# Three feed-forward stages run their first gate block on x before the norm's factor, and GpSimd forms low parts of weights

## The reference

```python
mod = c_act @ mod_w[i] + mod_b[i]                 # nine rows of 1024: shift, scale, gain, three times
h = modulate(rmsnorm_2(x, norm_g[i, 0]), sh1, sc1)   # h * (1 + scale) + shift
x = x + FFN_RES * g1[:, None, :] * swiglu_2(h, ffn_w13[i, 0], ffn_w2[i, 0])

def swiglu_2(h, w13, w2):
    a, b = jnp.split(h @ w13, 2, axis=-1)
    return (jax.nn.silu(a) * b) @ w2
```

## Time and profile before

| | us |
|---|---|
| device time, median of 3 runs | 1616.53 (1615.57 to 1620.67) |
| profiled execution, span | 1619.2 |
| PE busy | 1605.0 (99%) |
| DVE busy | 1221.3 (75%) |
| ACT busy | 807.2 (50%) |
| POOL busy | 48.4 (3%) |

### The profile page before, as it was taken

One profiled execution on the slowest core, in us unless ns is written; L12 is line 12 of the kernel. 1 busy time (PEld: TensorE's weight loads), 2 busy tenths in 40 slices (PEclk: granted clock), 3 DMA queues, 4 the chain that ended last, 5 costly groups with the idle time before them and its releaser, 6 DMA issues.

```text
span 1619.2 us, 33790 instructions
## 1 busy us (share of the span) xinstructions
PE 1605.0 (99%) x14157; PEld 1583.5 (98%) x14157; DVE 1221.3 (75%) x1382; ACT 807.2 (50%) x892; POOL 48.4 (3%) x81
## 2 busy tenths in 40 slices
PE   9999999999999999999999999999999999999998
PEld 9999999999999999999998999999999998899998
DVE  6888786676778878887777888877889578774544
ACT  5434567654644354443567654445444466654343
POOL 0000000000000000000000000000000010000000
PEclk9999999999999999999999999999999999999999
DMA  8788544444568865888453368874798535345551
GB/s 327 289 305 306 219 175 171 150 156 160 184 255 294 311 224 209 316 326 295 153 183 130 131 246 327 304 292 160 288 342 316 195 139 197 135 157 206 183 197 63
DMA packets 51066, 365.04 MB, mean 225 GB/s; under 512 B 5792, under 2 KB 5920, under 8 KB 7072
## 3 DMA queue, kind: packets, MB, share of 16 engines
q1 hardware_dynamic: 40176, 287.03, 48.5%
q0 software_dynamic: 10368, 75.50, 12.8%
q10 hardware_dynamic: 432, 1.20, 0.2%
HBM read 362.65 MB, written 1.05 MB: 225 GB/s over the span
## 4 chain that ended last, share of the span: by engine, by line
PE 95%; DVE 2%; ACT 1%; DMA 1%; issue 1%; DVEq 0%; SPq 0%; ACTq 0%
PE bank L261 54%; PE bank L297 27%; PE bank L253 3%; PE bank L280 2%; PE bank L2149 1%; PE bank L384 1%; DVE wlo L192 1%; PE bank L395 1%; DMA raw<-stream_in 0%; PE bank L1652 0%; PE bank L429 0%; PE bank L2195 0%; PE bank L2101 0%; PE bank L2119 0%; PE bank L1130 0%
## 5 line engine op out<-in xcount | busy, mean ns | idle before, releaser
L261 PE MATMUL bank<-xh,whi 128*128 128x256 f32 x2608 | 725.3, 278 | 1.3 <-DVE wlo L192 1.3
L261 PE MATMUL bank<-xl,whi 128*128 128x256 f32 x2608 | 721.6, 277 | 0.0
L261 PE MATMUL bank<-xh,wlo 128*128 128x256 f32 x2608 | 721.5, 277 | 0.0
L192 DVE TENSOR_TENSOR wlo<-raw,whi 128x2048 fp32r<-128x2048 f32 x254 | 580.9, 2288 | 180.5 <-ACT whi L184 180.2
L184 ACT ACTIVATE whi<-raw 128x2048 fp32r<-128x2048 f32 x253 | 482.8, 1913 | 277.3 <-PE bank L261 166.4
L261 PEld LDWEIGHTS bank<-xh,whi 128*128 128x128 f32 x2608 | 489.9, 188 | 2.6 <-DVE wlo L192 1.7
L261 PEld LDWEIGHTS bank<-xl,whi 128*128 128x128 f32 x2608 | 490.3, 188 | 0.1
L261 PEld LDWEIGHTS bank<-xh,wlo 128*128 128x128 f32 x2608 | 489.9, 188 | 0.0
L297 PE MATMUL bank<-hid_hi,whi 128*128 128x256 f32 x1056 | 292.1, 277 | 0.0
L297 PE MATMUL bank<-hid_lo,whi 128*128 128x256 f32 x1056 | 291.6, 276 | 0.0
L297 PE MATMUL bank<-hid_hi,wlo 128*128 128x256 f32 x1056 | 291.6, 276 | 0.0
(11 more groups left out here) (392 smaller groups left out, 1842.8 us busy)
## 6 DMA issues: line engine op xcount, KB each, us to landing
raw<-stream_in SPq DMA_DIRECT2D x269, 1024.0 KB, 4.9
mod_raw<-mod_in POOLq DMA_DIRECT2D x72, 1024.0 KB, 7.6
params<-params_in SPq DMA_DIRECT2D x1, 1474.0 KB, 9.5
x<-x_in SPq DMA_DIRECT2D x2, 512.0 KB, 4.7
raw<-stream_in SPq DMA_DIRECT2D x2, 512.0 KB, 6.6
m_gsu<-sgu_in ACTq DMA_DIRECT2D x1, 1024.0 KB, 4.7
y_out<-y_tiles SPq DMA_DIRECT2D x4, 256.0 KB, 2.9
consts<-consts_in SPq DMA_DIRECT2D x1, 280.5 KB, 7.2
```

The costliest lines, as they stand in the source:

```text
L192: dve.tensor_tensor(wlo[:, s, :], raw[:, s, :], whi[:, s, :].bitcast(F32), ALU.subtract)\
L261: last = pe.matmul(out[:, m, :], (whi, wlo)[wp][:, s, k * 256 + m * P:k * 256 + m * P + P], (xh, xl)[ap][:, k, :], start=(k == 0 and j == ...
```

## The change

Stages 6, 7 and 9 (AHEAD) no longer norm x before the first gate block. ACT rounds x times the gain into uh, row by row, DVE forms the remainder ul, PE runs the first gate block on these two into ACC[0] and ACC[1]. Two more columns of uh hold the shift's two parts, so that columns 256 and 257 of the product give the shift's share. The mean of squares is one matmul with ones in the middle of that block, after a tree of additions on DVE; the reciprocal is taken over 256 columns. Then DVE forms the normed rows as before, now with both operands in SBUF, and the up block waits for them. The gate bank is multiplied by the factor at its eviction, and the shift's share is the silu's bias. The filler matmuls of these norms are gone.

POOL forms wlo of blocks F0+1, F0+2 and F0+3 in these stages, in place of DVE. Stage 7's tables come after the first hidden step. The groups move, since stage 7's gain and shift must be known earlier.

```diff
+AHEAD = (6, 7, 9)
-MOD_GROUPS = {0: 3, 1: 3, 2: 4, 3: 4, 4: 4, 5: 0}
-GAIN_AFTER_STORE = (7,)
+MOD_GROUPS = {0: 4, 1: 4, 2: 4, 3: 3, 4: 3, 5: 0}
+GAIN_AFTER_STORE = ()
...
+        (_, uh, ul) = region(u_gap=([P, 24, T], F32), uh=([P, KD, T + 32], F32R), ul=([P, KD, T], F32R))
...
         def act_split_halves(act, n):
+            if n in AHEAD:
+                act_split(act, first_block[n] + 1)
...
+        def dve_between_residuals(dve, n, b):
+            layer, j = MOD_OF[n]
+            if b == 1:
+                dve.wait_ge(sem("u_rounded"), (KD + 1) * u_index[n] + 1)
+                dve.tensor_tensor(uh[:, :, T + 1:T + 2], mod_col(layer, j).unsqueeze(2), uh[:, :, T:T + 1].bitcast(F32),
+                                  ALU.subtract).then_inc(sem("u_split"), 1)
+            if b >= 1:
+                dve_pair(dve, n, b - 1)
...
+        def act_ahead(act, n):
...
+            act.activation(uh[:, :, T:T + 1], shift.unsqueeze(2), ACT.Copy).then_inc(sem("u_rounded"), 1)
+            for b, (k0, k1) in enumerate(X_TILES):
+                act.wait_ge(sem("x_updated"), X_STEPS * (last_stage(n) + 1) - X_STEPS + b + 1)
+                act.activation(xm[:, k0:k1, :], x[:, k0:k1, :], ACT.Square, scale=D ** -0.5).then_inc(sem("x_squared"), 1)
+                for k in range(k0, k1):
+                    act.activation(uh[:, k, 0:T], x[:, k, :], ACT.Identity, scale=gmod[:, k:k + 1]).then_inc(sem("u_rounded"), 1)
+            act_root(act, n)
+            act_split(act, F0 + 2)
+            for k in range(KD):
+                act.wait_ge(sem("xn_ready"), ready_before[n] + k + 1)
+                act.activation(xh[:, k, :], xm[:, k, :], ACT.Identity, bias=shift[:, k:k + 1]).then_inc(sem("xn_rounded"), 1)
+            act_split(act, F0 + 3)
...
+        def pe_ahead_block(pe, n):
+            s = slot_of(first_block[n])
+            pe.wait_ge(sem("w_lo_ready"), first_block[n] + 1)
+            pe.wait_ge(sem("x_updated"), X_STEPS * (last_stage(n) + 1) - X_STEPS + 2)
+            pe.wait_ge(sem("u_split"), (KD + 1) * u_index[n] + 1)
+            for part in range(2):
+                for k in range(KD):
+                    pe.wait_ge(sem(("u_rounded", "u_split")[part]), (KD + 1) * u_index[n] + k + 2)
...
+                if part == 0:
+                    pe.wait_ge(sem("x_paired"), paired_before[n] + N_PAIRS + 3)
+                    pe.matmul(STAT[:, 0:T], ones, xm[:, 0, :], start=True, stop=True, skip_group_check=True)\
+                      .then_inc(sem("x_summed"), 1)
...
+        def dve_ahead(dve, n):
...
+            dve_tree(dve, n, 0, 2, 3)
+            remainders(0, 2)
+            dve_pair(dve, n, 3)
+            dve_tree(dve, n, 4, 6, 5)
+            dve_tree(dve, n, 0, 4, 6)
+            remainders(2, 5)
+            dve.wait_ge(sem("std_ready"), norm_index[n] + 1)
+            dve.reciprocal(rstd[:, :], std[:, :]).then_inc(sem("rstd_ready"), 1)
+            remainders(5, 8)
...
+            for m in range(2):
+                dve.tensor_reduce(shift_cols[:, m:m + 1], ACC[m][:, T:T + 2], AX.X, ALU.add).then_inc(sem("bank_scaled"), 1)
+                dve.tensor_tensor(gate[:, m, :], ACC[m][:, 0:T], rstd[:, :], ALU.mult).then_inc(sem("bank_scaled"), 1)
+
+        def pool_first_splits(pool, n):
+            for b in range(first_block[n] + 1, first_block[n] + 4):
+                s = slot_of(b)
+                pool.wait_ge(sem("w_lo_ready"), b)
+                pool.wait_ge(sem("w_hi_ready"), b + 1)
+                pool.tensor_tensor(wlo[:, s, :], raw[:, s, :], whi[:, s, :].bitcast(F32), ALU.subtract)\
+                    .then_inc(sem("w_lo_ready"), 1)
...
             post(F0 + 1, S0, 0)
+            if n == TABLES_AT:
+                dve_tables(dve)
+            if n in AHEAD:
+                dve.wait_ge(sem("w_lo_ready"), F0 + 4)
...
+            first = n in AHEAD
+            if first:
+                turn(0, False, False)
             if groups:
                 with dve.Fori(0, groups) as i:
-                    turn(i, True, False)
+                    turn(i, True, False, int(first))
```

More of the change, by code:

```diff
@@ new lines, in dve_tree @@
+        def dve_tree(dve, n, to, of, pairs):
+            dve.wait_ge(sem("x_paired"), paired_before[n] + pairs)
+            dve.tensor_tensor(xm[:, to, :], xm[:, to, :], xm[:, of, :], ALU.add).then_inc(sem("x_paired"), 1)
+        def act_ahead(act, n):
+            layer, j = MOD_OF[n]
+            shift = mod_col(layer, j)
+            F0 = first_block[n]
+            act.activation(std[:, 8:9], cols[:, 64:65], ACT.Sqrt)
+            act.wait_ge(sem("gmod_ready"), 2 + sum(m < n for m in MOD_OF))
+            act.activation(uh[:, :, T:T + 1], shift.unsqueeze(2), ACT.Copy).then_inc(sem("u_rounded"), 1)
[10 more added lines that the diff above has]
+            act_split(act, F0 + 3)
@@ new lines, in pe_ahead_block @@
+        def pe_ahead_block(pe, n):
[7 more added lines that the diff above has]
+                    for m in range(2):
+                        c = k * 256 + m * P
+                        if part == 0:
+                            for w in (whi, wlo):
+                                pe.matmul(ACC[m][:, 0:T + 2], w[:, s, c:c + P], uh[:, k, 0:T + 2],
+                                          start=(k == 0 and w is whi), stop=False, skip_group_check=True)
+                        else:
+                            last = pe.matmul(ACC[m][:, 0:T], whi[:, s, c:c + P], ul[:, k, :], start=False,
+                                             stop=(k == KD - 1), skip_group_check=True)
+                if part == 0:
+                    pe.wait_ge(sem("x_paired"), paired_before[n] + N_PAIRS + 3)
+                    pe.matmul(STAT[:, 0:T], ones, xm[:, 0, :], start=True, stop=True, skip_group_check=True)\
+                      .then_inc(sem("x_summed"), 1)
+            last.then_inc(sem("w_used"), 1)
@@ L908, in round_hidden @@
                 act.activation(hid_hi[:, parity], hid[:, :, :], ACT.Copy).then_inc(sem("hid_rounded"), 1)
-            silu(F0)
-            act_split(act, F0 + 3)
-            if n == TABLES_AT:
-                act_tables(act)
-            round_hidden(S0, 0)
+            if n in AHEAD:
+                act.wait_ge(sem("bank_scaled"), 2 * STEPS * len(FACTOR_LATER) + 4 * u_index[n] + 4)
+                for m in range(2):
+                    ins = act.activation(gate[:, m, :], gate[:, m, :], ACT.Silu, bias=shift_cols[:, m:m + 1])
+                ins.then_inc(sem("silu_done"), 1)
+                round_hidden(S0, 0)
+                if n == TABLES_AT:
+                    act_tables(act)
+            else:
+                silu(F0)
+                act_split(act, F0 + 3)
+                round_hidden(S0, 0)
             def turn(i, last):
```

142 lines of the change are left out of this document (92 added, 50 removed).

## The result

The kernel after takes 1667.0 us in the median of 4 runs (1661.7 to 1671.2), against 1618.6 for the kernel before on the same chip (1615.6 to 1621.1): a ratio of 1.0301, 95% interval 1.0274 to 1.0328. The forecast was 1663.0. The profiled execution has a span of 1667.2 us, 48.0 more than that of the earlier trace rows.

The account below looks back on a forecast made before the run. PE, busy 99% of the span, was taken as the bound, so late data is paid in full. 9.9 + 9.8 + 9.8 + 3.9 + 13.1 = 46.5 us, added to 1616.5, gave 1663.0; range 1629 to 1674.

Parts of the forecast that it names:

- The forecast case: Whole kernel: GpSimd and VectorE hold each other, tables and groups add waits; +46.5 us to 1663.0, chance 55%.
- those of the stretches ahead of the loops: Ahead of the loops of stages 6, 7 and 9: +9.9, +13.7 and +9.8 us.
- the two folds: Ends of stages 0 and 2: the fold waits for the fourth group's sum; +6.8 and +6.3 us.
- The bound: Norm before the first gate block: DVE's chain ends last in place of PE's 5.33 us gap.
- part 1: Gap and first gate block: with every engine free, 1.3 us won in a stage, not 5.3.
- Part 2, the hold: GpSimd's three weight blocks, 4.5 us each, hold DVE; +9.9 us in one stage, +9.8 in each of two others.
- rival A: Early stages: back-to-back DVE instructions leave POOL no opening, delaying its second block; +5.0 us a stage, 1650 in all, chance 20%.
- Part 3, the tables: Stage 7: rope tables, 6.2 us of DVE behind the first hidden step, delay the first out block; +3.9 us.
- Part 4, the groups: Stages 0 and 2: a fourth group puts DVE 1.84 us behind per turn and its sum late; +13.1 us.
- The clock: Half clock after PE's waits in the new first blocks and behind late folds: 0 to 12 us, taken as 0.
- the second stand: PE's second 4.8 us wait in each new first block; DVE's pace doesn't hide the clock loss behind it in two stages.

Follow-up runs that it names:

- memset kernel: Kernel after with GpSimd's three subtractions in each of stages 6, 7 and 9 replaced by writing a constant into the same tile; 1644.5 us.
- The copy: Kernel after with GpSimd's three subtractions in each of stages 6, 7 and 9 replaced by a one-input copy of the weights; 1647.1 us.
- the GpSimd-free kernel: Kernel after with the three early low parts formed by VectorE and nothing on GpSimd; 1648.3 us, ratio 1.0182.
- the kernel before with 3, 3, 5, 4, 3: Kernel before with modulation groups 3, 3, 5, 4, 3 instead of 3, 3, 4, 4, 4 in the feed-forward stages; 1623.4 us, ratio 1.0008.
- after again: Kernel after run once more, unchanged; 1669.6 us, ratio 1.0292.
- groups-5 kernel: Kernel after with modulation groups 3, 3, 5, 4, 3 instead of 4, 4, 4, 3, 3 in the feed-forward stages; 1650.4 us, ratio 1.0192.

## Why the prediction was right, step by step

The forecast case came true, with the sum at 46.5 against 48.0 us. That it came so close is luck. Three of its terms, those of the stretches ahead of the loops, were too high by 7.7 us together (2.8, 1.1 and 3.8), though the measured stretches even hold 4.1 us of half clock that the sum had at nothing. Stage 7's loop, in which I forecast nothing, took 8.3 us, and the two folds 2.0 more than their term.

**The bound** was right: DVE's chain ends last in place of PE's gap. The memset kernel, the nearest to "nothing in the way", has -0.1 and -0.2 us, where part 1 forecast -1.3; it still waits 1.5 us for ul and has the lower clock behind that wait.

**Part 2, the hold.** Counted from the start of PE's first possible matmul of stage 6, E' = 942.52 in the kernel after:

| step | forecast | measured |
|---|---|---|
| PE starts the early block | E + 1.4 | 944.07, E' + 1.55 |
| reciprocal ends | E + 9.5 | 951.95, E' + 9.4 |
| second POOL block | E + 9.9 to 14.4 | 952.10 to 956.61, E' + 9.6 to 14.1 |
| DVE done with xl | 7 of 8 at E + 21.2 | 8 of 8 at 963.63, E' + 21.1 |
| third POOL block | E + 21.2 to 25.7 | asked 962.97, runs to 968.09, E' + 25.6 |
| up block ends | E + 26.4 | 965.97, E' + 23.5 |

Four of the six steps are within 0.3 us, the price of POOL's work too: 4.5 us taken, 4.50 to 4.60 measured for the six that had nothing to wait for. The step that failed is which DVE instruction the third POOL block holds. I had it ahead of the eighth remainder, which would have ended at E + 21.6 without a hold; DVE was there 0.5 us sooner, and POOL came in behind it. The hold then fell on gres, which PE doesn't wait for. By the forecast's own numbers the up block then ends at E + 21.9, which is +5.3 in place of +9.9. Measured are 7.1 in stage 6, of which 1.8 are the half clock, and 6.0 in stage 9, of which 1.3 are. One instruction of 0.4 us decided on 4.5 us, and no rival of mine stood for that: rival A has nearly this price, +5.0 a stage, but for another reason, that POOL's second block is put off, and that one came when forecast. The copy and the GpSimd-free kernel show that the hold is the cause of most of it, 7.1 to 2.5 and to 2.4 us.

**Part 3, the tables.** Right in kind; 13.7 forecast for the whole stage, 12.6 measured. The third hold does count in this stage, since gres, the scaling, the hidden rows and the tables stand behind it on DVE, but it comes out of a different place than I had it: DVE's chain is as forecast, the first out block starts at E' + 40.5 (forecast E + 40.9), while PE, with its up block done earlier, was ready for it at 34.1 and not at 37.1. 6.8 us of the 12.6 go when the tables move, against 3.9 forecast for them.

**Part 4, the groups.** Right: 13.1 forecast from the turns' lengths, 15.1 measured in the kernel after, 15.9 with nothing else changed. The terms were 1.84 us a turn and the late sum; transposes were forecast near 193 us and stand at 192.37. The wait itself is what I had; what is above it is mostly the clock, which costs the 24 matmuls behind a fold 0 to 2.5 us from one execution to another (the loops of the table at 6.4, 8.0 and 8.7).

**The clock**, which I took as 0 and bounded at 12, was 1.8, 1.0 and 1.3 us in the up blocks of stages 6, 7 and 9, 2.7 in the first out block of stage 7 and 2.5 behind one fold: some 9 us. The reason I gave for zero, that no row shows the filler's absence, was no reason: a term that is open between 0 and 12 is not 0, and I had written myself that DVE's pace doesn't hide the second stand in two stages. The earlier trace rows had shown a clock of 0.50 in a thin stretch, and I should have taken a middle value.

**Not in the forecast**: the slow loop, 5.7 us. It doesn't need the change, since the kernel before with 3, 3, 5, 4, 3 has it too; whether the change makes it more frequent is open.

## What to carry to other kernels

A shorter wait on one engine is worth what the next chain leaves of it: write the new chain of every engine with clock times before moving work, here DVE's remainders, reciprocal and products against PE's 5.3 us gap. Work given to GpSimd beside a busy VectorE is not free if it reads SBUF: where VectorE's next instruction has two SBUF inputs, it costs VectorE up to the whole of GpSimd's longer time, 4.5 us here for 2.3. A list of costs by turn (34.5 against 32.6 us) tells how many extra pieces a loop can carry before its last one comes late.

## What the runs showed of the hardware

- VectorE instructions with two SBUF inputs stood for the whole of a GpSimd operation that reads SBUF (uh 3.13 us, ul 4.7, unheld 0.17 and 0.48), and not for a memset of 1.81 us; residual rows with one input from PSUM were not held. A tensor_scalar of 128x8 with one SBUF input was held by the memset too (1.24 us) and by the subtraction (4.57).
- The wait goes both ways: GpSimd's third subtraction shows 5.12 us, 0.6 more than the others, in which it waited for a VectorE instruction of 0.4 us to end, and it did get in between two back-to-back VectorE instructions.
- TensorE's fp32 matmuls of 256 columns run at one of two pitches at the same granted clock of 1.00, 276 ns (48 in 5.44 us) or 281 ns (5.65). A feed-forward loop that ran at the slow one did so to its end and cost 6 us; such a loop turned up in 5 of the 14 executions whose traces were taken, in four different kernels. What sets it stays open: in the four traces looked through for it (before, after again, memset, groups 3, 3, 5, 4, 3 in before) the pitch never changed inside an unbroken row of these matmuls, only behind a wait, a change of clock or matmuls of another form; a bf16 matmul alone was followed by the slow pitch at 1163 us in the kernel after and at 1470 us in the groups-5 kernel, and by the fast one in most other places.
- The kernel before ranges over 12 us in its 23 runs beside its version with 3, 3, 5, 4, 3 (1615.3 to 1627.7), and a loop at the slow pitch is the size of step that would make such a spread. Only for the one profiled execution of 1627.4 us is it shown.
- PE's waits of 2.8 to 6.4 us in the kernel after were followed by a granted clock of 0.50 (some 2 us of it in stage 7's up block, 4 in stage 6's, 5 behind the fold of stage 0), but for the fold of stage 2, which saw none; 24 matmuls at a fold took 5.42, 4.55 or 2.94 us in different loops.
